# Two of three attentions in another order: every second step runs values, transposes, scores

## The reference

```
def mla_attention(q, k, v):
    ...
        s = jnp.einsum('bqhd,bkhd->bhqk', qi, k,
                       preferred_element_type=jnp.float32) * scale
        q_chunk = (i * Q_BLOCK + jnp.arange(Q_BLOCK)) // CHUNK_2
        mask = key_chunk[None, :] <= q_chunk[:, None]
        s = jnp.where(mask[None, None], s, NEG_INF)
        p = jax.nn.softmax(s, axis=-1).astype(v.dtype)
        return jnp.einsum('bhqk,bkhd->bqhd', p, v)
```

## Time and profile before

| | us |
|---|---|
| median of 3 runs | 1183.92 |
| lowest and highest | 1183.64, 1183.92 |
| the profiled execution | 1183.62 |
| its span, first to last instruction | 1181.9 |
| attention 2 (660.4 to 705.5 of the span) | 45.1 |
| attention 3 (725.2 to 777.7) | 52.5 |

### The profile page before, as it was taken

The page is one execution under the profiler, slowest core; times in us unless marked ns, Lnnn a source line. Parts: engine busy times, 40 slices in busy tenths (PEclk is TensorE's granted clock), DMA queues, the critical chain, the costliest instruction groups (busy, mean ns, idle before and its releaser), DMA issues.

```text
span 1181.9 us, 16137 instructions
## 1 busy us (share of the span) xinstructions
PE 1174.7 (99%) x5968; PEld 961.5 (81%) x5968; DVE 585.7 (50%) x1150; ACT 507.6 (43%) x794; POOL 455.0 (38%) x181
## 2 busy tenths in 40 slices
PE   9999999999999999999999999999999999999998
PEld 7887778988888888888988667689888888888887
DVE  4376455977777774112574567825434334340000
ACT  5443453634443432322646576834533443432110
POOL 6451314344434433444534210314434434434442
PEclk9999999999999999999999999999999999999999
DMA  8232122654554443223432110212232232223222
GB/s 305 86 110 105 36 97 83 214 183 177 209 206 172 189 156 102 91 94 111 143 129 72 54 37 1 72 36 73 107 107 85 93 106 106 73 72 98 98 98 95
DMA packets 27570, 132.38 MB, mean 112 GB/s; under 512 B 3456, under 2 KB 4608, under 8 KB 18688
## 3 DMA queue, kind: packets, MB, share of 16 engines
q1 hardware_dynamic: 25632, 129.22, 31.1%
q10 hardware_dynamic: 1888, 2.49, 0.7%
HBM read 129.60 MB, written 2.10 MB: 111 GB/s over the span
## 4 chain that ended last, share of the span: by engine, by line
PE 97%; DVE 1%; ACT 1%; POOL 0%; issue 0%; DMA 0%; DVEq 0%; ACTq 0%
PE psum L1513 86%; PE psum L1594 2%; PE psum L1582 2%; PE psum L2023 1%; PE psum L1743 1%; PE psum L1937 1%; PE psum L1836 1%; PE psum L1959 1%; POOL wl L479 0%; ACT prob L679 0%; DVE prob L1208 0%; DMA gains_and_h<-x_first 0%; PE psum L1801 0%; PE psum L1967 0%; DVE prob L1226 0%
## 5 line engine op out<-in xcount | busy, mean ns | idle before, releaser
L463 POOL TENSOR_TENSOR wl<-raw,wh 128x2048 fp32r<-128x2048 f32 (+2 forms) x89 | 365.7, 4109 | 510.1 <-ACT wh L602 285.2
L1513 PE MATMUL psum<-xh,wh 128*128 128x512 f32 (+1 forms) x1016 | 386.0, 380 | 0.1
L1513 PE MATMUL psum<-xl,wh 128*128 128x512 f32 (+1 forms) x1016 | 381.8, 376 | 0.0
L1513 PE MATMUL psum<-xh,wl 128*128 128x512 f32 (+1 forms) x1016 | 381.7, 376 | 0.0
L1159 DVE SCALAR_TENSOR_TENSOR scratch<-psum,cols,scratch 128x511 f32<-128x511 f32 (+1 forms) x176 | 131.7, 748 | 196.3 <-ACT scratch L740 188.0
L1513 PEld LDWEIGHTS psum<-xh,wh 128*128 128x128 f32 x1016 | 191.1, 188 | 40.1 <-issue 3.5
L1513 PEld LDWEIGHTS psum<-xh,wl 128*128 128x128 f32 x1016 | 191.1, 188 | 34.7
L1513 PEld LDWEIGHTS psum<-xl,wh 128*128 128x128 f32 x1016 | 191.2, 188 | 34.3 <-issue 0.2
L602 ACT ACTIVATE wh<-raw 128x2048 fp32r<-128x2048 f32 (+1 forms) x50 | 88.4, 1767 | 246.5 <-PE psum L1513 246.5
L1513 PE MATMUL psum<-acth,wh 128*128 128x512 f32 (+1 forms) x374 | 141.0, 377 | 0.0
L1513 PE MATMUL psum<-actl,wh 128*128 128x512 f32 (+1 forms) x374 | 140.8, 377 | 0.0
(11 more groups left out here) (262 smaller groups left out, 1388.6 us busy)
## 6 DMA issues: line engine op xcount, KB each, us to landing
raw<-stream SPq DMA_DIRECT2D x69, 1024.0 KB, 4.8
ada_raw<-ada SPq DMA_DIRECT2D x48, 512.0 KB, 5.2
raw<-down SPq DMA_DIRECT2D x32, 704.0 KB, 4.0
outT<-gains_and_h SPq DMA_DIRECT2D x8, 256.0 KB, 5.2
gains_and_h<-xT SPq DMA_DIRECT2D x7, 256.0 KB, 5.7
raw<-stream SPq DMA_DIRECT2D x7, 256.0 KB, 6.5
rel<-rel_tiles ACTq DMA_DIRECT2D x1, 1344.0 KB, 9.3
raw<-stream SPq DMA_DIRECT2D x2, 512.0 KB, 3.9
```

Of the source, the lines that this page charges most:

```text
L463: pool.tensor_tensor(wl[slot][:, 0:w], raw[slot][:, 0:w], wh[slot][:, 0:w].bitcast(F32), ALU.subtract).then_inc(lo_done, 1)
L1513: ins = pe.matmul(out, lhs[a], rhs[b], start=first and n == 0, stop=last and n == 2)
```

## The change

Attentions 2 and 3 alone are changed; attention 1 runs as before.

- TensorE: even steps run S(n), beside, T(n-3), V(n-5). Odd steps run V(n-5), beside, T(n-3), S(n). From step 16 on the order is the old one, and the last step has V(14) and V(15).
- ScalarE: step n runs C(n-3), E(n-1) where it ran C(n-3), E(n). The copy of a finished pair comes one step later.
- VectorE: step n runs I(n-2), N(n-2), M(n), R(n).
- `probT` has a third buffer in attentions 2 and 3, which takes the place of `sq2`; the squares of query heads take `scratch[2:4]` for the first two and `sq2` for the next.
- Two waits of TensorE on copied values stand at other steps.

The diff, in which "..." marks bodies that are only moved into functions:

```diff
--- before.py
+++ after.py
@@ -195,7 +195,9 @@
             ones64 = sb("ones64", [P, P], F32R, s)
-            sq2 = [sb(f"sq2{b}", [P, T], F32, s) for b in range(2)]
+            with ExitStack() as s2:
+                sq2 = [sb(f"sq2{b}", [P, T], F32, s2) for b in range(2)]
+            probT2.append(sb("probT22", [P, 2, T], F32, s))
             sqk = [sb(f"sqk{b}", [P, T], F32, s) for b in range(2)]
@@ -316,13 +318,13 @@
         QUERY_SUMS = bank[7]
-        square_q = sq2 + scratch[2:4]
+        square_q = scratch[2:4] + sq2
         EARLY = HEADS // 2
-        NORM_LAG = 1
         TURN_LAG = 3
         LAG = 4
+        LATE = 5
         NEXT_BANK = bank[3]
         TURN_BANKS = psum[:, 4:6, :]
@@ -337,6 +339,14 @@
         def unit(a, step):
             return a * STEPS + step
+        def values_of(a, step):
+            if a == 0:
+                return [step - LAG] if step >= LAG else []
+            if step == STEPS + LAG - 1:
+                return [STEPS - 2, STEPS - 1]
+            return [step - LATE] if step >= LATE else []
...
@@ -663,26 +673,30 @@
                 def turned(step):
                     V, w = unit(a, step - TURN_LAG), width(step - TURN_LAG)
                     act.wait_ge(att.pt, V + 1)
-                    if V >= 2:
-                        act.wait_ge(att.pv, V - 1)
-                    act.activation(probT[V % 2][:, :, 0:w], TURN_BANKS[:, :, 0:w], ACT.Copy).then_inc(att.ptc, 1)
+                    buffers = len(probT)
+                    if V >= buffers:
+                        act.wait_ge(att.pv, V - buffers + 1)
+                    act.activation(probT[V % buffers][:, :, 0:w], TURN_BANKS[:, :, 0:w], ACT.Copy).then_inc(att.ptc, 1)
+                lag = LAG if a == 0 else LATE
+                exp_lag = 0 if a == 0 else 1
                 for step in range(STEPS + LAG):
                     if TURN_LAG <= step < STEPS + TURN_LAG:
                         turned(step)
-                    if step < STEPS:
+                    if exp_lag <= step < STEPS + exp_lag:
+                        x = step - exp_lag
+                        V, w = unit(a, x), width(x)
                         for e in range(2):
...
-                                           scale=minus_rq[:, 2 * step + e:2 * step + e + 1] if a == 2 else -1.0,
+                                           scale=minus_rq[:, 2 * x + e:2 * x + e + 1] if a == 2 else -1.0,
                                            accum_out=row_sum[:, c:c + 1]).then_inc(att.exp, 1)
                     if beside is not None:
                         beside(step)
-                    if step > TB + LAG - 1 and (step - LAG) % TB == 0:
-                        heads_high(a, (step - LAG) // TB - 1)
+                    if step > TB + lag - 1 and (step - lag) % TB == 0:
+                        heads_high(a, (step - lag) // TB - 1)
                 heads_high(a, PAIRS - 1)
@@ -1195,37 +1209,49 @@
             def attend(a, prob, neg_max, row_sum, col0, before=None, beside=None, after=None):
+                def maxima(step):
+                    V, w, c = unit(a, step), width(step), col0 + 2 * step
+                    if V >= 4:
...
+                        dve.tensor_tensor_reduce(prob[V % 4][:, e, 0:w], scores_banks(a, V)[e][:, 0:w], bias[:, T - w:T],
+                                                 -1.0, FAR, ALU.add, ALU.min, neg_max[:, c + e:c + e + 1]).then_inc(att.raw if a == 2 else att.max, 1)
+                def inverse(x):
+                    V, c = unit(a, x), col0 + 2 * x
+                    dve.wait_ge(att.exp, 2 * V + 2)
+                    dve.reciprocal(row_sum[:, c:c + 2], row_sum[:, c:c + 2]).then_inc(att.rinv, 1)
+                def scaled(x):
+                    V, w, c = unit(a, x), width(x), col0 + 2 * x
+                    dve.wait_ge(att.rinv, V + 1)
+                    dve.tensor_scalar(prob[V % 4][:, 0, 0:w], prob[V % 4][:, 0, 0:w], row_sum[:, c:c + 1], None, ALU.mult).then_inc(att.norm, 1)
+                    dve.tensor_scalar(prob[V % 4][:, 1, 0:w], prob[V % 4][:, 1, 0:w], row_sum[:, c + 1:c + 2], None, ALU.mult).then_inc(att.norm, 1)
+                lag = LAG if a == 0 else LATE
                 for step in range(STEPS + LAG):
+                    v = step - (1 if a == 0 else 2)
+                    if a and 0 <= v < STEPS:
+                        inverse(v)
+                        scaled(v)
                     if step < STEPS:
                         if before is not None:
                             before(step)
...
-                    norming = NORM_LAG <= step < STEPS + NORM_LAG
-                    if norming:
-                        v = step - NORM_LAG
...
-                        if a == 2:
-                            now = col0 + 2 * step
-                            dve.wait_ge(att.raw, 2 * step + 2)
-                            dve.tensor_tensor(neg_max[:, now:now + 2], neg_max[:, now:now + 2], rq[:, 2 * step:2 * step + 2], ALU.mult).then_inc(att.max, 2)
-                        if beside is not None:
-                            beside(step)
-                    if norming:
-                        dve.wait_ge(att.rinv, V + 1)
-                        dve.tensor_scalar(prob[V % 4][:, 0, 0:w], prob[V % 4][:, 0, 0:w], row_sum[:, c:c + 1], None, ALU.mult).then_inc(att.norm, 1)
-                        dve.tensor_scalar(prob[V % 4][:, 1, 0:w], prob[V % 4][:, 1, 0:w], row_sum[:, c + 1:c + 2], None, ALU.mult).then_inc(att.norm, 1)
-                    if step > TB + LAG and (step - LAG - 1) % TB == 0:
-                        heads_low(a, (step - LAG - 1) // TB - 1)
+                        maxima(step)
+                    if a == 0 and 0 <= v < STEPS:
+                        inverse(v)
+                    if a == 2 and step < STEPS:
+                        now = col0 + 2 * step
+                        dve.wait_ge(att.raw, 2 * step + 2)
+                        dve.tensor_tensor(neg_max[:, now:now + 2], neg_max[:, now:now + 2], rq[:, 2 * step:2 * step + 2], ALU.mult).then_inc(att.max, 2)
+                    if step < STEPS and beside is not None:
+                        beside(step)
+                    if a == 0 and 0 <= v < STEPS:
+                        scaled(v)
+                    if step > TB + lag and (step - lag - 1) % TB == 0:
+                        heads_low(a, (step - lag - 1) // TB - 1)
@@ -1552,39 +1578,43 @@
                 pe.matmul(SS_BANKS[j][:, half(j)], ones[:, :], ss_acc[:, half(j)], start=True, stop=True).then_inc(norm.ss, 1)
             def attend(a, ready, scores, decays, v, prob, probT, ident, beside=None):
-                for step in range(STEPS + LAG):
-                    if step < STEPS:
-                        V, p, i, w = unit(a, step), step // TB, step % TB, width(step)
-                        outs = scores_banks(a, V)
-                        ready(step)
-                        if a == 0 and step:
...
+                def scores_step(step):
+                    if step >= STEPS:
+                        return
+                    V, p, i, w = unit(a, step), step // TB, step % TB, width(step)
+                    outs = scores_banks(a, V)
+                    ready(step)
...
+                    if decays is not None:
                         for e in range(2):
-                            ins = scores(p, i, e, outs[e], w)
-                            if decays is None:
-                                ins.then_inc(att.qk, 1)
-                        if decays is not None:
-                            for e in range(2):
-                                decays(p, e, outs[e], w).then_inc(att.qk, 1)
-                    if beside is not None:
-                        beside(step)
-                    if TURN_LAG <= step < STEPS + TURN_LAG:
-                        V, i = unit(a, step - TURN_LAG), (step - TURN_LAG) % TB
-                        pe.wait_ge(att.norm, 2 * V + 2)
-                        if V >= 1:
...
-                    if step >= LAG:
-                        V, p, i = unit(a, step - LAG), (step - LAG) // TB, (step - LAG) % TB
+                            decays(p, e, outs[e], w).then_inc(att.qk, 1)
+                def turn_step(step):
+                    if not TURN_LAG <= step < STEPS + TURN_LAG:
+                        return
+                    V, i = unit(a, step - TURN_LAG), (step - TURN_LAG) % TB
...
+                def values_step(step):
+                    for x in values_of(a, step):
+                        V, p, i = unit(a, x), x // TB, x % TB
                         pe.wait_ge(att.ptc, V + 1)
-                        if a == 1 and step == LAG:
+                        if a == 1 and x == 0:
...
-                                                probT[V % 2][:, e, P * j:P * j + P], start=j == 0, stop=j == i)
+                                                probT[V % len(probT)][:, e, P * j:P * j + P], start=j == 0, stop=j == i)
+                for step in range(STEPS + LAG):
```

(33 more changed lines are left out.)

36 lines of the change are left out of this document (12 added, 24 removed).

## The result

The changed kernel takes 1188.72 us (median of 6 runs, 1186.09 to 1189.64), the kernel before 1183.78 us beside it: a ratio of 1.0040, 95% interval 1.0029 to 1.0051. It is 0.4% slower, clear of what a measurement can tell. The profiled execution took 1189.64 us, with a span of 1187.9.

A forecast was written before the change was run, and what follows sets the result against it. TensorE, busy 1174.7 of 1181.9 us, was taken as the bound. A gain of 4.6 us against added waits of 5.6 (attention 3) and 2.7 (attention 2) gave +3.7 on 1183.92: 1187.5 us, range 1182.0 to 1189.0.

The forecast's parts named there:

- gain, attention 2: TensorE in attention 2: 34 changes of array shape in place of 47, saving 2.2 us.
- gain, attention 3: TensorE in attention 3: 19 shape changes in place of 31, and T behind V slightly cheaper, saving 2.4 us.
- waits, attention 2: TensorE's waits in attention 2 grow to 4.0 us in place of 1.3, adding 2.7 us.
- waits, attention 3: TensorE's waits in attention 3 grow to 8.0 us in place of the walk's 2.4, adding 5.6 us.
- two V stand together without a price: Paired values on TensorE: no left-over between two V, taken as nothing within bounds of 0 to 0.15 us per pair.
- T6 and T10: Attention 3: these transposes each wait 2.2 us for scalings N6 and N10, held by GpSimd's subtractions.
- The 0.4 at T7 and T11: Attention 3: GpSimd's hits on scalings N7 and N11 add 0.4 us of wait at these transposes.
- T0, T2, T4: Attention 3: these transposes wait 0.9, 0.9 and 0.8 us behind longer chains on VectorE and ScalarE.
- the collision: VectorE scalings starting just behind a GpSimd subtraction wait for its end: 1.52 us in place of 0.41.
- the fourth rival: Longer chains than walked, a late weight chunk or TensorE's clock falling in the waits: over 1189 us, chance 0.04.
- Rival 3: GpSimd's subtractions miss the scalings in attentions 2 and 3, ScalarE waits stay: 1182.9 us, chance 0.17.
- rival 2: Attention 3: GpSimd meets only the second half of N6 and N10, T6 waits 0.8 us: 1184.9 us, chance 0.08.

The follow-up runs named there:

- experiment 1: GpSimd's subtractions beside attentions 2 and 3 cut into sixteen pieces instead of four: changed kernel 1183.63 us, kernel before with the same cut 1183.23 us.
- the other scaling: Changed kernel with the scalings of attentions 2 and 3 written as scalar_tensor_tensor instead of tensor_scalar: 1196.53 us, ratio 1.0101 to the kernel before.
- step 1 as before: Changed kernel with step 1 of attention 3 in the old order on TensorE, S1 ahead of the last query product: 1187.03 us, ratio 1.0026.

## Why the prediction was right, and where it was not

**Sign, mechanism and range** were right: forecast 1187.5 us (1182.0 to 1189.0), measured 1188.72, slower. That the sum came so near, and that the median lies 0.3 us inside the range, is partly luck: two errors ran against each other, waits forecast too long and spells left out. Its terms, measured from start to start in the profile, with the waits counted as what a block took beyond its length elsewhere:

| term, us | forecast | measured |
|---|---|---|
| gain, attention 2 | -2.2 | -2.6 |
| gain, attention 3 | -2.4 | -2.4 |
| waits, attention 2 | 4.0 in place of 1.3: +2.7 | 3.4 in place of 0.8: +2.5 |
| waits, attention 3 | 8.0 in place of 2.4: +5.6 | 6.7 in place of 2.0: +4.8 |
| spells at half clock | 0, and 0.04 for a case over 1189 | +3.2 in the profiled run |

**Without the spells** the measured terms add up to +2.3: 1186.1 us. The one run of the changed kernel at a clock of 1.000 took 1186.09. The forecast of 3.7 for these terms was 1.4 too high.

**The gain.** That two V stand together without a price, which had no row, is right (1.28 us against 1.40 apart); the net time of attention 3 is 50.6 us before (52.56 less 1.95 of waits) and 48.2 after (58.16 less 6.74 of waits and 3.24 of spells).

**T6 and T10.** Forecast 2.2 us each, measured 1.9, by the mechanism and at the moment that the prediction gave; experiment 1 shows that GpSimd is its cause. The 0.4 at T7 and T11 was too much: 0.2 at T7, and at T11 nothing that can be told from the spell, since S13 and S14, at half clock, cover N11.

**T0, T2, T4.** Forecast 0.9, 0.9 and 0.8; measured 1.0, 0.7 and 0.8, with the releasers named. **Attention 2:** T2 (with V0 ahead of it) 1.3 in place of 1.4, T6 1.2 in place of 1.4, the others 0.1 to 0.3 where 0.1 to 0.4 were forecast. The prediction applied the collision to the scalings alone; R meets it too (0.62 us at 752.11 in place of 0.16), on which the change itself did not turn.

**The step that failed** is in the fourth rival. It named a fall of TensorE's clock in the waits, and waved it off with the clock of 1.00 in every stretch of the earlier trace rows, idle 0.7 us included. Those stretches had no wait of the length that the prediction itself was forecasting; rows with 0.7 us of idle could not speak for a wait of 2.2 us, nor even for T0's 0.85. A spell costs 1.5 to 1.7 us, and two of them lifted the profiled run to 1189.64, above the range. Five of the six runs are below a clock of 1.000 and three lie above 1189.0, so a price of nothing and a chance of 0.04 were too low.

**Rival 3** (no collision) was given 1182.9 us. With the collisions cut to tenths of a us the kernel takes 1182.0 to 1182.4 us at full clock, so the price was about right for a case that did not come. The terms that the prediction lists don't give it, though: the forecast less 5.1 us at T6, T7, T10 and T11 and less 1.0 in attention 2 is 1181.4. Two smaller sums are off by a little: the waits listed for attention 3 add up to 7.9, not 8.0, and in rival 2 a wait of 0.8 in place of 2.2 saves 1.4 us each, not 1.3.

## What to carry to other kernels

When an engine is to be relieved by a new order of its own work, walk the lists of all engines through a period with measured durations: here such a walk gave each of the rearranged attentions within 0.5 us wherever the clock held; for the changed kernel's attention 3 it gave 55.9 us, against 54.9 less the spells. Look for a tensor_scalar, or a VectorE instruction with two tensors from SBUF, that now starts just behind a GpSimd subtraction: here it waited for the rest of that piece, and one edit, smaller pieces, took most of the wait away. Where a change puts waits of a us or more in front of TensorE, allow for more than their length.

## What the runs showed of the hardware

- In the profiles the granted clock of TensorE fell to 0.50 for 3.3 to 3.4 us at a time, once for 6.7 us (the other scaling, 753.4 to 760.0). Each fall came between 1.5 us ahead of the end of one of TensorE's waits and 1.1 us behind it. The changed kernel had none to about two from run to run, and times fall into groups 1 to 2 us apart: 1184.9, 1186.9 to 1187.2, 1187.8 to 1188.8 for the one with step 1 as before.
- Held by the GpSimd subtraction under way were tensor_scalar (1.29 and 1.42 us in place of 0.41), scalar_tensor_tensor with two tensors in SBUF (3.05 for two in place of 1.15) and a tensor_tensor on two columns, both inputs in SBUF (1.10 in place of 0.16). Not held were a reciprocal on two columns of SBUF (0.17 us in the middle of a subtraction) and a maximum that reads its scores from PSUM (its usual 0.28 us).
- Cutting four GpSimd subtractions into sixteen made them longer in all: 7.37 us against 5.19 in the changed kernel, 6.95 against 5.17 in the kernel before, 0.15 to 0.18 us for each piece more.
